# Down products of two of three feed-forward groups as seven block products, with GpSimd forming part of the activations' sums and most low parts

## The reference, cut to what matters

```python
def swiglu_ffn(x, w13, w2):          # x: (1, 528, 1024), w13: (1024, 2*2752), w2: (2752, 1024)
    a, u = jnp.split(x @ w13, 2, axis=-1)
    return (jax.nn.silu(a) * u) @ w2
```

## Time and profile before

| | |
|---|---|
| median of 3 runs | 3070.95 us (3065.07 to 3071.05) |
| span of the profiled execution | 3068.8 us |
| TensorE matmul busy | 2951.0 us, 96% |
| VectorE busy | 1685.5 us, 55% |
| ScalarE busy | 1211.2 us, 39% |
| GpSimd busy | 969.8 us, 32% |

### The profile page before, as it was taken

The page is one execution under the profiler, slowest core; times in us unless marked ns, Lnnn a source line. Parts: engine busy times, 40 slices in busy tenths (PEclk is TensorE's granted clock), DMA queues, the critical chain, the costliest instruction groups (busy, mean ns, idle before and its releaser), DMA issues.

```text
span 3068.8 us, 58164 instructions
## 1 busy us (share of the span) xinstructions
PE 2951.0 (96%) x24214; PEld 2525.6 (82%) x24214; DVE 1685.5 (55%) x2762; ACT 1211.2 (39%) x2299; POOL 969.8 (32%) x687
## 2 busy tenths in 40 slices
PE   7999899989999979999999999999999999999998
PEld 5678788654444459999998999999999999889996
DVE  4257755632222256847483568557666465477583
ACT  3154423210000045535524546346454443374463
POOL 1030367100000024233563433344332365343332
PEclk9999999999999999999999999999999999999999
DMA  7541100379999952222221123232232222113321
GB/s 304 223 133 56 70 3 3 134 296 418 429 428 428 428 209 89 97 95 105 84 83 56 56 97 111 83 107 79 104 111 76 97 86 80 56 70 110 110 81 51
DMA packets 38516, 440.08 MB, mean 143 GB/s; under 512 B 6136, under 2 KB 6776, under 8 KB 12026
## 3 DMA queue, kind: packets, MB, share of 16 engines
q1 hardware_dynamic: 36824, 435.29, 36.2%
q10 hardware_dynamic: 1448, 1.31, 0.2%
HBM read 433.69 MB, written 2.11 MB: 142 GB/s over the span
## 4 chain that ended last, share of the span: by engine, by line
PE 58%; DVE 2%; ACT 2%; issue 1%; POOL 0%; DVEq 0%; ACTq 0%
PE PS L3189 23%; PE PS L3057 23%; PE PS L3054 4%; PE PS L3068 2%; PE PS L3590 2%; PE PS L2645 1%; PE PS L3625 1%; PE PS L2651 1%; PE PS L3608 1%; ACT w_hi L2986 0%; DVE t_lo L3160 0%; ACT h_hi L2867 0%; PE PS L2658 0%; ACT low L2870 0%; PE PS L3585 0%
## 5 line engine op out<-in xcount | busy, mean ns | idle before, releaser
L2999 POOL TENSOR_TENSOR w_lo<-low,w_hi 128x512 fp32r<-128x512 f32 (+4 forms) x310 | 629.7, 2037 | 1498.0 <-ACT w_hi L2986 1492.8
L2986 ACT ACTIVATE w_hi<-low 128x512 fp32r<-128x512 f32 (+3 forms) x670 | 485.6, 744 | 475.0 <-PE PS L3057 290.3
L3189 PE MATMUL PS<-t_hi,w_hi 128*128 128x264 f32 (+1 forms) x1152 | 327.1, 284 | 7.9 <-ACT low L3263 7.9
L3189 PE MATMUL PS<-t_hi,w_lo 128*128 128x264 f32 (+1 forms) x1152 | 327.6, 284 | 0.0
L3189 PE MATMUL PS<-t_lo,w_hi 128*128 128x264 f32 (+1 forms) x1152 | 326.2, 283 | 0.0
L3004 DVE TENSOR_TENSOR w_lo<-low,w_hi 128x512 fp32r<-128x512 f32 x360 | 258.4, 734 | 32.1 <-ACT w_hi L2986 30.9
L3189 PE MATMUL PS<-h_hi,w_lo 128*128 128x264 f32 (+1 forms) x864 | 244.8, 283 | 0.0
L3189 PE MATMUL PS<-h_hi,w_hi 128*128 128x264 f32 (+1 forms) x864 | 244.5, 283 | 0.4 <-issue 0.4
L3189 PE MATMUL PS<-h_lo,w_hi 128*128 128x264 f32 (+1 forms) x864 | 244.8, 283 | 0.0
L2232 PE MATMUL PS<-arena 128*64 128x512 f32 x1024 | 225.8, 594 | 13.7 <-DMA arena<-wts_dram 13.6
L3057 PE MATMUL PS<-g_hi,w_hi 128*128 128x264 f32 x1056 | 231.0, 286 | 1.2 <-DVE high L3451 1.2
(11 more groups left out here) (490 smaller groups left out, 6742.9 us busy)
## 6 DMA issues: line engine op xcount, KB each, us to landing
arena<-wts_dram SPq DMA_DIRECT2D x99, 2048.0 KB, 19.5
low<-wts_dram SPq DMA_DIRECT2D x77, 2048.0 KB, 7.8
arena<-wmod_dram SPq DMA_DIRECT2D x9, 2048.0 KB, 9.0
low<-wts_dram SPq DMA_DIRECT2D x12, 1536.0 KB, 6.4
arena<-na_bias_dram SPq DMA_DIRECT2D x16, 512.0 KB, 3.5
arena<-wts_dram SPq DMA_DIRECT2D x4, 1024.0 KB, 17.9
high<-tab_dram SPq DMA_DIRECT2D x1, 2225.0 KB, 30.1
arena<-x_cols_dram SPq DMA_DIRECT2D x1, 2048.0 KB, 8.6
```

What stands on the lines that cost most here:

```text
L2986: nc.scalar.activation(hi, raw, ACT.Copy).then_inc(w_h.sem, 1)
L2999: nc.gpsimd.tensor_tensor(lo, raw, hi.bitcast(F32), ALU.subtract).then_inc(w_lp.sem, 1)
L3189: last = nc.tensor.matmul(PS[:, b, 0:n], wt[wi][:, k, :], xs[xi], start=(i in (0, 1, 3) and k == 0 and j == 0), stop=(k == 3 and j == 2), ...
```

## The change

The groups become 7, 7 and 8 tiles. In the first two, the down stage works on pairs `p` = 0 to 3 of output tiles. Of the group's seven tiles, the first six form a contraction of 3 + 3 tiles; with two output tiles and two halves of tokens that is a 2 x 2 by 2 x 2 block product, done by seven block products of 3 x 3 = 9 matmuls each; the seventh tile is multiplied plainly (`PLAIN`, 12 matmuls). A pair is 7 x 9 + 12 = 75 matmuls of 264 columns (256 in the last feed-forward). The third group keeps its plain down stage. Sums of weights (384 columns) are VectorE's as in the tiles. Of the eight items of a pair VectorE makes the low parts of 1 and 2, GpSimd of the six others. The sums of activations t1 (VectorE, while tiles 0 to 2 of the group are gated), t2 (VectorE), t3 and t4 (GpSimd) and the sums' low parts (GpSimd) are made for k = 0, 1, 2 while TensorE multiplies the fifth, sixth and seventh tile of the group. `t3_sb`, `t24l_sb` and so on are their semaphores. Raw weights come in chunks of half the size, 1 MB, one tile or pair each, in two slots; the mixer's weights too.

```diff
-GROUPS = [(0, 6), (6, 8), (14, FT - 14)]
-DNC = 2
-FFNC = W13C + DNC * len(GROUPS)
+GROUPS = [(0, 7), (7, 7), (14, FT - 14)]
+NPAIR = DK // 2
+FFNC = FT + NPAIR * len(GROUPS)
 RAW = 2
+SLOT2 = 2048
...
+PAIR = 3 * P
+PLAIN = 7
+PAIR_ORDER = (0, 1, 3, 2, 5, 4, PLAIN, 6)
+ITEM_AT, SET_WIDTH = [], []
...
+DOWN_PAIR = (4 * PAIR + 2 * P, 8)
...
-ON_VECTOR = [p[4] is not None and p[4][1] in (1, *SUMMED) for p in PIECES]
+ON_VECTOR = [p[4] is not None and p[4][1] in ((1, *SUMMED) if SET_WIDTH[p[4][0]] == ITEM else (1, 2)) for p in PIECES]
...
+    b_lo = f32r("b_lo", RAW * SLOT2, GD, L)
+    t24_hi = [f32r("t24_hi_0", RAW * SLOT2 + GD * L, 1, L)[:, 0, :], g_hi[:, GF - 1, :], g_lo[:, GF - 1, :]]
...
+    PAIR_STEPS = [(0, 0), (0, 1)]
+    PAIR_OUT = [(0, "x1")]
+    for p in range(NPAIR):
+        PAIR_STEPS += [(p, 3), (p, 2)] + [(p + 1, 0)] * (p + 1 < NPAIR) + [(p, 5), (p, 4)] + [(p + 1, 1)] * (p + 1 < NPAIR) + [(p, PLAIN), (p, 6)]
+        PAIR_OUT += [(p, "y4"), (p, "x3")] + [(p + 1, "x1")] * (p + 1 < NPAIR) + [(p, x) for x in ("x5", "z", "y", "w", "x")]
...
+    def pairs_pe(pe, l, w, g, fin):
+        f0, nf = GROUPS[g]
+        h0, h1, n = tokens_of(0, fin), tokens_of(1, fin), width(fin)
+
...
+        for p, x in PAIR_STEPS:
+            bank_x, bank_y, bank_z, bank_w = (pair_bank(g, p, b) for b in range(4))
+            wt = [v.rearrange("p (k n) -> p k n", n=P) for v in weights(pe, l, ITEM_AT[pair_set(w, g, p)][x])]
+            if x == 0:
+                if p == 0:
+                    gl_sb.wait(pe, l, w * FT + f0 + GD)
+                if p < 2:
+                    sl_sb.wait(pe, l, w * FT + f0 + GD + p)
+                    c21_sb.wait(pe, l, seventh(w, f0 + GD - 1 + p) + 1)
+                else:
+                    pair_taken(pe, l, w, g, p - 2, "x")
+            elif p == 0 and x == 3:
+                t3l_sb.wait(pe, l, sum_at(w, g, 2) + 1)
+            elif p == 0 and x in (2, 5):
+                t24l_sb.wait(pe, l, sum_at(w, g, 2) + 1)
+            elif p == 0 and x == 4:
+                t1l_sb.wait(pe, l, sum_at(w, g, 2) + 1)
+            if x == 2:
+                pair_taken(pe, l, w, g, p, "x1")
+            elif x == 5:
+                pair_taken(pe, l, w, g, p, "y4")
+            elif x == 4:
+                pair_taken(pe, l, w, g, p, "x3")
+            elif x == PLAIN:
+                if p == 0:
+                    gl_sb.wait(pe, l, w * FT + f0 + nf)
+                for b, m, h in ((bank_w, 1, h1), (bank_z, 0, h0), (bank_y, 1, h0)):
+                    last = three(b, [v[:, m, :] for v in wt], (g_hi[:, GD, h], g_lo[:, GD, h]), b == bank_w, True)
+                pair_taken(pe, l, w, g, p, "x5")
+                last = three(bank_x, [v[:, 0, :] for v in wt], (g_hi[:, GD, h1], g_lo[:, GD, h1]), False, False)
...
+            last.then_inc(dv_ps.sem, 1)
+
...
+        def third_sum_high(g, k):
+            t3_sb.wait(act, l, sum_at(w, g, k) + 1)
+            nc.scalar.activation(b_lo[:, k, h1], g_32[:, k, h1], ACT.Copy).then_inc(t3h_sb.sem, 1)
+
+        def other_sums_high(g, k):
+            t2_sb.wait(act, l, sum_at(w, g, k) + 1)
+            t4_sb.wait(act, l, sum_at(w, g, k) + 1)
+            nc.scalar.activation(toks(t24_hi[k], fin), toks(g_32[:, 3 + k, :], fin), ACT.Copy).then_inc(t24h_sb.sem, 1)
 
...
+            if before is not None and before < 3:
+                after[5].append((first_sum_high, g, before))
+            elif before is not None:
+                after[4].append((third_sum_high, g, before - 3))
+                after[6].append((other_sums_high, g, before - 3))
 
...
+        def third_sum(g, k):
+            g_sb.wait(pool, l, w * FT + GROUPS[g][0] + 3 + k + 1)
+            t1_sb.wait(pool, l, sum_at(w, g, k) + 1)
+            nc.gpsimd.tensor_tensor(g_32[:, k, h1], g_32[:, 3 + k, h1], g_32[:, k, h1], ALU.subtract).then_inc(t3_sb.sem, 1)
+
+        def fourth_sum(g, k):
+            t2_sb.wait(pool, l, sum_at(w, g, k) + 1)
+            nc.gpsimd.tensor_tensor(g_32[:, 3 + k, h0], g_32[:, 3 + k, h0], g_32[:, 3 + k, h1], ALU.subtract).then_inc(t4_sb.sem, 1)
+
+        def first_sum_low(g, k):
+            t2_sb.wait(pool, l, sum_at(w, g, k) + 1)
+            t1h_sb.wait(pool, l, sum_at(w, g, k) + 1)
+            nc.gpsimd.tensor_tensor(g_lo[:, k, h0], g_32[:, k, h0], g_hi[:, k, h1].bitcast(F32), ALU.subtract).then_inc(t1l_sb.sem, 1)
+
+        def third_sum_low(g, k):
+            t3h_sb.wait(pool, l, sum_at(w, g, k) + 1)
+            nc.gpsimd.tensor_tensor(g_lo[:, k, h1], g_32[:, k, h1], b_lo[:, k, h1].bitcast(F32), ALU.subtract).then_inc(t3l_sb.sem, 1)
+
+        def other_sums_low(g, k):
+            t24h_sb.wait(pool, l, sum_at(w, g, k) + 1)
+            nc.gpsimd.tensor_tensor(toks(g_lo[:, 3 + k, :], fin), toks(g_32[:, 3 + k, :], fin), toks(t24_hi[k].bitcast(F32), fin),
+                                    ALU.subtract).then_inc(t24l_sb.sem, 1)
+
...
+        for g, (f0, nf) in enumerate(GROUPS):
+            for f in range(max(f0, F_SEVEN[0]), min(f0 + nf, FT - 1)):
+                last = f == f0 + nf - 1
+                if f + 1 == FT - 1:
+                    continue
+                at = [i for i in sorted(ITEM_AT[pair_set(w, g, 0) if last else tile_set(w, f + 1)].values()) if not ON_VECTOR[i]]
+                sums = paired_group(g) and f - 1 - f0 in range(3, GD)
+                k = f - 4 - f0
+                split_pool(pool, l, at[0])
+                if sums:
+                    third_sum(g, k)
+                    fourth_sum(g, k)
+                for i in at[1:-3]:
+                    split_pool(pool, l, i)
+                if sums:
+                    third_sum_low(g, k)
+                    first_sum_low(g, k)
+                for i in at[max(1, len(at) - 3):]:
+                    split_pool(pool, l, i)
+                if sums:
+                    other_sums_low(g, k)
+            if paired_group(g):
+                for p in range(1, NPAIR):
+                    for i in sorted(ITEM_AT[pair_set(w, g, p)].values()):
+                        split_pool(pool, l, i)
+                for x in range(7):
+                    split_pool(pool, l, ITEM_AT[tile_set(w, f0 + nf)][x])
...
+            j = f - f0
+            src = g_full(f, f0) if f < FT - 1 else gs[:, f % 2, :]
+            dst = b_lo[:, j, :] if in_pairs(f) else g_lo[:, j, :]
+            ts = h0 if in_pairs(f) and j < 3 else slice(NMETA if fin else 0, L)
+            nc.vector.tensor_tensor(dst[:, ts], src[:, ts], g_hi[:, j, ts].bitcast(F32), ALU.subtract).then_inc(gl_sb.sem, 1)
+            if not in_pairs(f):
+                return
+            gl_sb.wait(dve, l, w * FT + f + 1)
+            g = group_of(f)
+            if j < 3:
+                nc.vector.tensor_tensor(g_32[:, j, h0], g_32[:, j, h1], g_32[:, j, h0], ALU.subtract).then_inc(t1_sb.sem, 1)
+            else:
+                t3_sb.wait(dve, l, sum_at(w, g, j - 3) + 1)
+                nc.vector.tensor_tensor(g_32[:, j, h1], g_32[:, j, h1], g_32[:, j - 3, h0], ALU.subtract).then_inc(t2_sb.sem, 1)
 
...
+            def pair_out(p, name):
+                b, step, m, h = OUT_OF[name]
...
+                pair_stepped(dve, l, w, g, p, step)
...
+                x = res[:, 2 * p + m, (h0, h1)[h]]
+                nc.vector.scalar_tensor_tensor(x, PS[:, pair_bank(g, p, b), 0:wide], 0.5, x, ALU.mult, ALU.add).then_inc(dv_sb.sem, 1)
+
...
+                pair_out(0, "x1")
+                for p in range(NPAIR):
+                    more = p + 1 < NPAIR
+                    q = pair_set(w, g, p) + 1
+                    weight_sum_1(dve, l, q)
+                    pair_out(p, "y4")
+                    pair_out(p, "x3")
+                    weight_sum_3(dve, l, q)
+                    if more:
+                        pair_out(p + 1, "x1")
+                    split_vector(dve, l, ITEM_AT[q][1])
+                    weight_sum_2(dve, l, q)
+                    pair_out(p, "x5")
+                    weight_sum_4(dve, l, q)
+                    split_vector(dve, l, ITEM_AT[q][2])
+                    for name in ("z", "y", "w"):
+                        pair_out(p, name)
+                    if not more:
+                        low_item(f, 3)
+                    pair_out(p, "x")
+                low_item(f, 4, 6)
```

369 lines of the change are left out of this document (233 added, 136 removed).

## The result

The changed kernel takes 3154.73 us (median of 4 runs, 3152.16 to 3159.01) beside 3070.57 us (3065.07 to 3071.05) for the kernel before: ratio 1.028, 95% interval 1.0266 to 1.0296. It is slower, as forecast, and 22 us slower than the 3133 forecast. The profiled execution, with a span of 3157.1 us, is the slowest of the four (3159.01 us). From here on the lines are those of the changed kernel: 3254 are the tiles' matmuls, 3278 those of the pairs, 3408 ScalarE's kept copies out of PSUM (before 3263), 3390 its copy of the gate's high part (before 3258), 3047, 3052, 3058 and 3064 VectorE's four sums, 3027 its low parts, 3022 those of GpSimd, 3544 GpSimd's low parts of t2 and t4.

The account below looks back on a forecast made before the run. TensorE, 96% busy, was taken to bound the kernel, with VectorE and GpSimd's shared load just behind. Span 3068.8 - 33.3 + 96 = 3131.5 us, so 3133 as median; range 3060 to 3172.

Parts of the forecast that it names:

- Matmuls removed, -33.3 us: In the down stages of the first two groups, fewer matmuls save 33.3 us in sum, if nothing stalls.
- Shared load: GpSimd's instructions and VectorE's with two SBUF inputs exclude each other, so times add: 78.2 us a group against TensorE's 67.2.
- Where the stalls lie: TensorE waits 3.5 and 3.2 us in sixth and seventh tiles, about 5 at pair 0's item 2, 1 between pairs.
- Size, 12 us a group: Added stall taken for each of eight groups, between bounds of 7 and 16 us: 96 us in all.
- the walk: Following a group instruction by instruction with the listed prices, which gave 14 us of stalls a group.
- the sum of loads, 11.0: From a group's fifth tile on, shared load exceeds TensorE's time by 11.0 us, by plain addition.
- The clock, 0: Longer waits could lower TensorE's clock; set to 0, since the page shows full clock through waits of 3 us.
- The third group keeps its length: Listed as a sign that the forecast is right: the third group's length stays unchanged.
- Chunks 0: Weight loads of 1 MB land in 5.1 us, within some 7 us of cover, so they cost 0.
- mostly absorbed load: Rival: the shared load costs only 7 us a group, giving 3094 us; chance 0.12 for 3077 to 3105.
- the other side: Rival: GpSimd's added work fits VectorE's holes, giving 3038 to 3062 us; chance 0.21 with its border, 0.15 below 3065.
- waits that feed on each other: Rival: stalls of 16 us a group plus late chunks of 2 each, giving 3182 us; chance 0.07 above 3165.

Follow-up runs that it names:

- the one with short fills: Changed kernel with GpSimd's five subtractions for the sums of activations each replaced by a single fill with zeros: 3069.22 us, ratio 1.0008 to the kernel before.
- experiment 3: Changed kernel with GpSimd's five subtractions replaced by repeated zero fills, keeping GpSimd about as busy without reading SBUF: 3077.01 us, ratio 1.0034 to the kernel before.
- experiment 4: Kernel before with only the 1 MB weight chunks of the change, products and groups as before: 3068.32 us, ratio 0.9997.
- experiment 6: Changed kernel with t3, t4, the sums' low parts and the pairs' low parts of items 0, 3, 4, 6 moved to VectorE: 3103.06 us, ratio 1.0111.

## Why the prediction came out as it did

The forecast was slower, by 62 us; it is 84. By its steps:

- **Matmuls removed, -33.3 us: consistent with the runs, not isolated.** After the stalls the pairs' matmuls follow each other as before, 35 in 4 us. No run has the pairs without any stall; the one with short fills has down stages of 38.5 us with 1.3 us of waits between pairs; less these and two restarts of 0.27 that is 36.7, close to the 36.5 of the sum.
- **Shared load: right, and shown.** With the reads of the five subtractions gone (experiment 3) 78 of the 84 us between the medians are gone. By the note in the Trainium skill's page "Advanced Engine Details and Errata" (VectorE Performance Modes, Mode Summary), which names the two-port modes alone, that run and the changed kernel should have been alike. The prediction took this note for what the whole page says; elsewhere that page of the Trainium skill names two SBUF inputs as well (Miscellaneous Facts, GPSIMD Details). The 78 us side with "SBUF — State Buffer" of the Trainium skill (Who interferes with whom), by which GpSimd instructions that only write do not contend with VectorE's that read SBUF twice.
- **Where the stalls lie: right, the seventh tile smaller.** Item 2 of pair 0 waits 4.0 us (forecast about 5) for the instruction named; pairs wait 0.66 us, two a group (forecast 1 at two or three places); in the sixth and seventh tile the kept copies wait 2.6 and 1.2 us (forecast 3.5 and 3.2): 1.39 and 1.22 us, 1.01 and 0.20 us, in the first group of the second feed-forward.
- **Size, 12 us a group: too small for the whole, too large for the waits.** The whole is (88.3 + 33.3) / 8 = 15.2. The waits alone, of which the walk was made, are 84.3 / 8 = 10.5: below the 12 taken and the walk's 14, and near the sum of loads, 11.0. What carries the measured time beyond the forecast is what no term of the sum held: the half clock (17.9 us) and the restarts (16.4), 4.3 us a group. In spans the forecast is 25.6 us short: 34.3 left out and 3 open, less 11.7 of waits set too high. That these partly cancel is luck. The argument for the 12, that a sum of loads has no idle in it, was not borne out here; it is right in that an engine that is behind also waits for others (GpSimd 2.39 us for t2 in the timeline above). A small slip: the 2.41 us for one piece of 1024 columns is not in the earlier trace rows, which show two in 4.75; it changes the prices by 0.02 us at most.
- **The clock, 0: wrong.** This is the largest term missing, 17.9 us. I took the page's row of tenths for proof that waits of 3 us leave the clock alone. That row can't show it: a half-clock stretch of 7 us in a slice of 77 us stays a 9. And the kernel before has no such waits in its layers. From 1150 us on TensorE's longest is 1.7 us, but for one of 3.2 at 3060.07 us,

```profile
PE PS L3943 <- DVE high L2750: 3.2, 1, 3.2
```

  and there the granted clock is 0.50 in every window of 2 us from 3054 to 3064 us. Windows of 2 us around the waits of 4 us show the same in the changed kernel.
- **The restart after a wait, not in the sum: 16.4 us.** The forecast priced waits by their idle time alone.
- **The third group keeps its length: nearly.** 73.55 us for seven tiles against 71.7. The first tile after each down stage of pairs, in the second group too, waits 1.2 to 1.5 us for a kept copy, eight times in all:

```profile
1888.77 1.15 ACT L3009 ACTIVATE w_hi<-low 128x512 fp32r<-128x512 f32 x2 [2.24 <-DVE low L3058]
1889.82 0.37 ACT L3408 ACTIVATE low<-PS 128x264 f32<-128x264 f32 x1
```

  It is the second of the two roads, which the walk had left out: the copy behind high parts that wait for a weight sum. In the kernel before, this tile's sums were made in a long plain down stage with little to do; now they follow the last pair's. The last sentence is read from the order of the work, no run tests it.
- **Chunks 0: right** (experiment 4, within 0.12% below and 0.07% above). **ScalarE 0: right as a load** (41% busy, 39% before), but its fixed order carries most of the waits.
- **Mixer 0: right.** From the first matmul of each feed-forward to the end of its last seven-product tile the changed kernel takes 22.0, 20.5, 22.8 and 24.2 us more, 89.4 together, where the spans differ by 88.3. The stretches between them, with the last down stage and the mixer, differ by 0.2 us or less.
- **Rivals.** The mostly absorbed load (3094) and the other side (below 3065) failed by the shared load; waits that feed on each other (16 us a group and late chunks, 3182) come near the 15.2 a group only as a number: the waits are 10.5, the chunks' part is missing, and 3182 is further from 3154.7 than the forecast.

No version beat the kernel before. The best complete one (experiment 6, the sums and all but two of a pair's low parts on VectorE) is 1.1% slower than it (1.0094 to 1.0127), and even with GpSimd's sums as fills it only ties.
